# A transformer pair in float32 on one core: nine-instruction roots, a gather of 96 columns, and the gate row of each feed forward at its end

## What is computed

```python
def modulate(x, g, shift, scale):
    return rmsnorm(x, g) * (1.0 + scale) + shift

x = x + g1 * o
x = x + g2 * swiglu(modulate(x, n_ffn, sh2, sc2), wg, wu, wd)

def swiglu(h, wg, wu, wd):
    return (jax.nn.silu(h @ wg) * (h @ wu)) @ wd
```

## Time and profile before

| | |
|---|---|
| median of 3 runs | 2700.8 us (2697.67 to 2712.5) |
| profiled execution: its time, its span | 2701.12 us, 2698.8 us |
| PE busy, share of the span | 2443.1 us, 91% |
| DVE busy | 1892.0 us, 70% |
| ACT busy | 1472.7 us, 55% |
| HBM read | 671.79 MB |
| TensorE clock granted, mean | 0.957 |

### The profile page before, as it was taken

How to read it: one execution, slowest core, us unless ns; L and a number is a source line. 1 busy time by engine, 2 the same in 40 slices (tenths; PEclk the granted TensorE clock), 3 DMA queues, 4 the chain that set the end, 5 groups by cost and what they waited for, 6 DMA issues and landing times. The chain is left out here.

```text
span 2698.8 us, 58018 instructions
## 1 busy us (share of the span) xinstructions
PE 2443.1 (91%) x22896; PEld 1854.2 (69%) x22998; DVE 1892.0 (70%) x2521; ACT 1472.7 (55%) x1865; POOL 14.9 (1%) x12
## 2 busy tenths in 40 slices
PE   5978999999888879989999999898999999999997
PEld 4745777677664457768677768567777777777775
DVE  3277555555545566555666555669999999999997
ACT  3146444443321545433454434358887888888885
POOL 0000000000200000000000000000000000000000
PEclk9989999999798899999799999789999999999999
DMA  7340555554466126545375545339999999999995
GB/s 293 116 202 24 225 204 195 210 209 148 148 230 244 61 98 250 206 179 201 118 265 196 208 158 207 113 138 357 414 415 403 418 416 413 418 417 418 418 417 227
DMA packets 121210, 674.35 MB, mean 250 GB/s; under 512 B 13488, under 2 KB 13968, under 8 KB 67088
## 3 DMA queue, kind: packets, MB, share of 16 engines
q1 hardware_dynamic: 120032, 664.47, 63.6%
q10 hardware_dynamic: 1072, 8.42, 0.9%
HBM read 671.79 MB, written 1.05 MB: 249 GB/s over the span
## 5 line engine op out<-in xcount | busy, mean ns | idle before, releaser
L959 PE MATMUL ps<-projected,normed_or_mix 128*128 128x256 bf16 x1504 | 409.9, 273 | 1.2 <-issue 1.2
L960 PE MATMUL ps<-projected,normed_or_mix 128*128 128x256 bf16 x1504 | 409.9, 273 | 0.0
L1345 DVE TENSOR_TENSOR aux<-weights,aux 128x1024 bf16<-128x1024 f32 x224 | 273.2, 1220 | 1.4 <-ACT aux L1289 1.4
L1340 DVE TENSOR_TENSOR normed_or_mix<-weights,normed_or_mix 128x2048 bf16<-128x2048 f32 x111 | 254.4, 2292 | 15.5 <-ACT normed_or_mix L1283 10.5
L1340 DVE TENSOR_TENSOR turned<-weights,turned 128x2048 bf16<-128x2048 f32 x112 | 256.6, 2291 | 7.0 <-ACT turned L1283 2.3
L1283 ACT ACTIVATE turned<-weights 128x2048 bf16<-128x2048 f32 x112 | 213.8, 1909 | 52.6 <-DMA weights<-moe 52.6
L1283 ACT ACTIVATE normed_or_mix<-weights 128x2048 bf16<-128x2048 f32 x111 | 212.0, 1910 | 50.8 <-DMA weights<-moe 48.1
L1213 PE MATMUL ps<-projected,normed_or_mix 128*128 (+1 forms) x1792 | 234.5, 207 | 3.3 <-DVEq L1370 3.3
L1289 ACT ACTIVATE aux<-weights 128x1024 bf16<-128x1024 f32 x224 | 233.5, 1043 | 2.1 <-PE ps L1227 1.8
L1214 PE MATMUL ps<-projected,normed_or_mix 128*128 (+1 forms) x1792 | 234.5, 207 | 0.0
L1215 PE MATMUL ps<-projected,normed_or_mix 128*128 (+1 forms) x1792 | 234.5, 207 | 0.0
(11 more groups left out here) (385 smaller groups left out, 5905.7 us busy)
## 6 DMA issues: line engine op xcount, KB each, us to landing
weights<-moe SPq DMA_DIRECT2D x224, 1024.0 KB, 8.5
weights<-moe SPq DMA_DIRECT2D x224, 512.0 KB, 6.6
weights<-l_ffn SPq DMA_DIRECT2D x66, 1024.0 KB, 5.2
weights<-ada SPq DMA_DIRECT2D x64, 1024.0 KB, 5.6
weights<-l_ffn SPq DMA_DIRECT2D x66, 512.0 KB, 5.5
weights<-ada SPq DMA_DIRECT2D x64, 512.0 KB, 6.1
weights<-ffn SPq DMA_DIRECT2D x28, 1024.0 KB, 5.1
weights<-w_in SPq DMA_DIRECT2D x24, 948.0 KB, 4.6
```

The costliest lines, as they stand in the source:

```text
L959: pe.matmul(o, hi, h_hi(k), start=(k == 0), stop=False)
L960: pe.matmul(o, hi, h_lo(k), start=False, stop=False)
L1340: dve.tensor_tensor(gu4[j % SLOTS][1], RING[:, slot(j), 0:2 * D], gu4[j % SLOTS][0], ALU.subtract).then_inc(front_used.sem, 1)
L1345: dve.tensor_tensor(down4[j % SLOTS][1], RING[:, slot(j), 2 * D:3 * D], down4[j % SLOTS][0], ALU.subtract).then_inc(back_used.sem, 1)
```

## The change

The root becomes nine instructions: a first guess with another constant, one Newton step with another factor, and a last step of higher order; the first of the nine is no longer awaited. `modulate` ahead of a feed forward no longer has `gates`. `ffn_parts` makes the gate row itself: PE's 8 matmuls go ahead of the last down, into banks 6 and 7, ACT copies them behind the last silu, and DVE waits for the copy before it multiplies the first bank. At a feed forward's head the order on ACT and DVE becomes input half, gate, input half, up; PE starts with the first half of the input and the gate, and the matmuls of the condition go ahead of the zeros. In the choice of experts the places are 96 instead of 128 (384 columns a gathering matmul instead of 512), and ACT and DVE cast the gate and up of step 1 and the down of step 0 there instead of in the block of the loop.

```diff
-GUESS = 1597463007.0
+GUESS = 1597815328.0
+ROOT = 1.5 ** 0.2
+NEAR = 1.5849084
...
     def rsqrt(dve, r, v, u):
 
-        dve_step(dve, dve.tensor_scalar(r.bitcast(I32), v.bitcast(I32), -0.5, GUESS, ALU.mult, ALU.add))
+        dve.tensor_scalar(r.bitcast(I32), v.bitcast(I32), -0.5, GUESS, ALU.mult, ALU.add)
         dve_step(dve, dve.tensor_scalar(v, v, -0.5, None, ALU.mult))
-        for i in range(3):
+        for near in (True, False):
             dve_step(dve, dve.tensor_tensor(u, r, r, ALU.mult))
             dve_step(dve, dve.tensor_tensor(u, u, v, ALU.mult))
-            last = dve.scalar_tensor_tensor(out=r, in0=u, scalar=1.5, in1=r, op0=ALU.add, op1=ALU.mult)
-            if i < 2:
-                dve_step(dve, last)
-        return last
+            if near:
+                dve_step(dve, dve.scalar_tensor_tensor(out=r, in0=u, scalar=NEAR, in1=r, op0=ALU.add, op1=ALU.mult))
+        dve_step(dve, dve.scalar_tensor_tensor(out=u, in0=u, scalar=ROOT ** 2 * 5 / 3, in1=u, op0=ALU.add, op1=ALU.mult))
+        return dve.scalar_tensor_tensor(out=r, in0=u, scalar=ROOT ** 4 * 1.25, in1=r, op0=ALU.add, op1=ALU.mult)
...
             for k in range(KD):
+                if by_half and w == 0 and k % (KD // 2) == 0:
+                    pe.wait_ge(S.h_lo.sem, S.h_lo.at(k // (KD // 2) + 1))
...
         def products(pe):
+            for i in range(ada_n):
+                ada_row(pe, i, ada_at)
             for bank in range(4):
                 pe.matmul(PS[:, bank, :], Z16[:, 0:PB], Z16[:, :], start=True, stop=False)
...
-            for i in range(ada_n):
-                ada_row(pe, i, ada_at)
             zero_products(pe, 2 if ada_n else 14, 5)
-            pe.wait_ge(S.h_lo.sem, S.h_lo.at(2))
+            if gates is not None:
+                pe.wait_ge(S.h_lo.sem, S.h_lo.at(2))
...
             for c in range(rounds * SLOTS, n):
                 if c + 1 < n:
                     up(c + 1, c + 1)
+                elif gates is None:
+                    pe.wait_ge(S.ada_out.sem, S.ada_out.at(ada_n))
+                    gate_products(pe, row_gates, 6)
                 down_products(pe, c, c, outs, stop=(c == n - 1), each=S.bank_done if c == n - 1 else None)
...
+            if gates is None:
+                keep_gate(act, 0, row_gates, 6)
             squares(act)
...
+            dve.wait_ge(S.gate_kept.sem, S.gate_kept.at(1))
             for b in range(2):
...
-    modulate([(X, 0, 3, 0), (XC, 0, 3, 1)], col("n_ffn", 0, KD), batch=1,
-             gates=[(gate_row, 0, 5, 0), (ctx_gate, 0, 5, 1)])
-    ffn(X, F0, 0)
-    ffn(XC, F0, T, ctx_gate, first=2)
+    modulate([(X, 0, 3, 0), (XC, 0, 3, 1)], col("n_ffn", 0, KD), batch=1)
+    ffn(X, F0, 0, (0, 5, 0))
+    ffn(XC, F0, T, (0, 5, 1), first=2)
...
-                        mm = pe.matmul(PS[:, 4 * part + q % 4, :], tok[:, b, k * PB:(k + 1) * PB],
+                        mm = pe.matmul(PS[:, 4 * part + q % 4, 0:4 * CAP], tok[:, b, k * PB:(k + 1) * PB],
...
                 make_lo(dve, 0, 0, 0)
+                dve.wait_ge(S.hi_gu.sem, S.hi_gu.at(2))
+                dve.tensor_tensor(second_gu[1], second, second_gu[0], ALU.subtract).then_inc(front_used.sem, 1)
+                dve.wait_ge(S.hi_d.sem, S.hi_d.at(1))
+                dve.tensor_tensor(first_down[1], back, first_down[0], ALU.subtract).then_inc(back_used.sem, 1)
                 dve.wait_ge(S.made.sem, S.made.at(1))
...
                 cast_hi(act, 0, 0, 0, free=False)
+                arrived(act, place.n + 1)
+                act.activation(second_gu[0], second, ACT.Copy).then_inc(S.hi_gu.sem, 1)
+                arrived(act, place.n)
+                act.activation(first_down[0], back, ACT.Copy).then_inc(S.hi_d.sem, 1)
```

More of the change, by code:

```diff
@@ L533, in mean_square, with gate_products @@
                                         op0=ALU.add, op1=ALU.add)
-    def gate_products(pe, gates):
+    def gate_products(pe, gates, bank=0):
         for g, (dst, layer, part, c) in enumerate(gates):
             for k in range(KD):
-                mm = pe.matmul(PS[:, 2 * g + k // 4, k % 4 * PB:(k % 4 + 1) * PB],
+                mm = pe.matmul(PS[:, bank + 2 * g + k // 4, k % 4 * PB:(k % 4 + 1) * PB],
                                ADA[:, layer, part * KD + k, c:c + 1].broadcast_to([PB, PB]), ident,
@@ L1009, in ffn_done, with ffn_parts @@
             s.done(n)
-    def ffn_parts(x, f, o, gates=None, gate=GB, first=0, ada_at=None, ada_n=0):
+    def ffn_parts(x, f, o, gates=None, own_gate=None, first=0, ada_at=None, ada_n=0):
         a, n = place.n, f // PB * (NE if gates is not None else 1)
@@ L1022, in ffn_parts @@
         halves = (slice(0, KD // 2), slice(KD // 2, KD))
+        gate, row_gates = GB, own_gate and [(GB[:, :], *own_gate)]
         def products(pe):
+            for i in range(ada_n):
+                ada_row(pe, i, ada_at)
             for bank in range(4):
@@ L1053, in silus @@
         def silus(act):
-            for half in halves:
+            for i, half in enumerate(halves):
                 act.activation(h_hi[:, half, :], h[:, half, :], ACT.Copy).then_inc(S.h_hi.sem, 1)
+                if gates is None and i == 0:
+                    act.wait_ge(front_in[place.n % SLOTS].sem, 16 * (place.n // SLOTS + 1))
+                    act.activation(gu[0][0][:, 0:D], RING[:, place.n % SLOTS, 0:D], ACT.Copy).then_inc(S.w_hi.sem, 1)
             if gates is None:
-                act.wait_ge(front_in[place.n % SLOTS].sem, 16 * (place.n // SLOTS + 1))
-                act.activation(gu[0][0][:, 0:D], RING[:, place.n % SLOTS, 0:D], ACT.Copy).then_inc(S.w_hi.sem, 1)
                 act.activation(gu[0][0][:, D:2 * D], RING[:, place.n % SLOTS, D:2 * D],
@@ L1154, in cast_hi_loop, with ffn @@
             act.activation(split[parity(j)][2][0], RING[:, s, 2 * D:3 * D], ACT.Copy).then_inc(S.hi_d.sem, 1)
-    def ffn(x, f, o, gate=GB, first=0):
+    def ffn(x, f, o, own_gate, first=0):
         a, n, beside = place.n, f // PB, 2
         place.n += beside
-        products, silus, gating = ffn_parts(x, f, o, gate=gate, first=first, ada_at=a, ada_n=beside)
+        products, silus, gating = ffn_parts(x, f, o, own_gate=own_gate, first=first, ada_at=a, ada_n=beside)
         with nc.Block() as block:
@@ L1300, in product_hi @@
                                ACT.Copy).then_inc(S.act_hi.sem, 1)
-            gate_up(1, 1, False)
-            down(0, 0, False)
             gate_up(2, 2, False)
@@ L1371, in gating @@
             dve.sem_inc(S.prod.sem, 2)
-            gate_up(1, 1)
-            down(0, 0)
             gate_up(2, 2)
@@ L2250, in gathered_tile @@
             half, k = q // KD, q % KD
-            return ((HEH, HEL)[part][:, 4 * half:4 * half + 4, k, :],
-                    PS[:, 4 * part + q % 4, :].rearrange("p (e q) -> p e q", e=4))
+            return ((HEH, HEL)[part][:, 4 * half:4 * half + 4, k, 0:CAP],
+                    PS[:, 4 * part + q % 4, 0:4 * CAP].rearrange("p (e q) -> p e q", e=4))
+        second_gu = [XC[:, h, :].bitcast(BF16) for h in range(2)]
+        first_down = [AUX[:, h * 512:(h + 1) * 512].bitcast(BF16) for h in range(2)]
+        second, back = RING[:, (place.n + 1) % SLOTS, 0:2 * D], RING[:, place.n % SLOTS, 2 * D:3 * D]
         with nc.Block() as block:
@@ L2379, in turn_put @@
                 for b in range(2):
[L2380 removed]
+                    t = pe.transpose(PS[0:CAP, e // 2, e % 2 * T + b * PB:e % 2 * T + (b + 1) * PB],
+                                     put[b][:, e, 0:CAP], ident)
                 if e % 2:
@@ L2396, in spread_gates, with move_casts @@
                     mm.then_inc(S.spread.sem, 1)
+            gate_products(pe, general_gate, 6)
             pe.wait_ge(S.spread_kept.sem, 4)
+        def move_casts(dve):
+            for h in range(2):
+                dve.tensor_copy(down[0][h], first_down[h]).then_inc(S.casts_moved.sem, 1)
+            dve.wait_ge(S.casts_moved.sem, 2)
+            for h in range(2):
+                dve.tensor_copy(gu[1][h], second_gu[h]).then_inc(S.casts_moved.sem, 1)
         def keep_spread(act):
+            act.wait_ge(S.casts_moved.sem, 4)
             for i in range(4):
```

49 lines of the change are left out of this document (28 added, 21 removed).

## The result

| | before | changed |
|---|---|---|
| median of 20 runs each | 2704.8 us | 2711.4 us |
| ratio of changed to before | | 1.0029, 95% interval 1.0020 to 1.0039 |
| span of the profiled execution | 2698.8 us | 2709.1 us |
| TensorE clock granted, mean | 0.957 | 0.946 |

A forecast was written before the change was run, and what follows sets the result against it. It took TensorE to bound the feed forwards and DMA of weights the expert loop; terms -2.0 - 2.1 + 8.8 - 1.4 - 0.2 - 2.0 = +1.1 gave 2702 us, range 2693 to 2711.

The forecast's parts named there:

- Step 1: Shorter roots: 0.5 us saved a root, four of sixteen on the path, -2.0 us.
- Step 2: Modulations without gate rows: transposes start sooner, -0.6 or -0.7 us each, -0.1 ahead of the experts; sum -2.1, bounds 0 and -4.
- The rival of the clock: TensorE's clock falls in heads behind longer pauses, about 2.4 us each; 2705 to 2707 with one or two; 15%.
- the heaviest case: Heads and modulations of three feed forwards and the experts' gather all at low clock: 14.4 us, 2716; 4% of the 15.
- a low clock in a head that had 2.4 GHz: Sign in the new profile that the prediction would be wrong.
- Step 3: Gate row ahead of the last down: first gate multiply 2.2 us later in each of four feed forwards, +8.8 us.
- Step 4: Feed forward heads by halves: 0.45 us sooner in each of three heads, -1.4 us in all.
- Step 5: Choice of experts: subtractions +3.3 us on the logits' chain, narrower gather -3.3, narrower copy and placement -0.2; sum -0.2.
- Step 6: Start of the expert weight stream: three loads may go at once instead of one, -2.0 us, bounds 0 and -3.8.

The follow-up runs named there:

- roots_alone: The kernel before with the shorter roots alone; ratio to before 0.9992 (0.9982 to 1.0002).
- gates_left_out: The kernel before without gate products and gate row copies in the three modulations ahead of the feed forwards, nothing in their place; ratio to before 1.0034.
- casts_back: The changed kernel with the two casts and two subtractions back at the start of the experts' loop; ratio to before 1.0053.
- unused_products: The changed kernel with gate products back in all four modulations, results unread, the gate row still made at the feed forward's end; ratio to before 1.0009.
- head_alone: The kernel before with only the new feed forward head (condition's products first, input and weights by halves); ratio to before 0.9992.
- gather128: The changed kernel with gather, picks and copies at 128 columns an expert again, casts and subtractions still early; ratio to before 1.0046.
- warm2: The changed kernel with gate rows back in the modulations, zero products in TensorE's pauses and six more ahead of the router's products; ratio to before 0.9957.

## Why the prediction was wrong, step by step

**Step 1, roots: right, as far as the runs can tell.** At the same place the stretch is 1.72 us for 2.25, so 0.53 a root for the 0.5 of the sum. In roots_alone the stretches that begin at three of the four roots are 0.52, 0.74 and 0.53 shorter; the fourth, ahead of the experts, shows 0.02 only. The runs give 2.2 us for 2.0, with an interval that reaches 1.

**Step 2, the modulations without gate rows: this is the step that failed.** It has -2.1 with 0 as its upper bound ("the transposes run at the lower clock instead"). gates_left_out, which does this step alone for the four feed forwards, measured +9.2. The bound looked only at the transposes. The clock stays low through the head behind them: in layer 1 of the changed kernel the 32 condition products cost 2.56 us more (5.35 for 2.79). The -0.1 ahead of the experts fails too: without the subtractions, casts_back still has the logits 3.5 us later, behind router products at 1.2 GHz. That the missing gate products are the whole cause there is not shown, since unused_products brings the stretch back only to +2.87.

**The rival of the clock had the mechanism, and was priced and weighed too low.** It gave 2705 to 2707 for one or two heads, 2716 for the heaviest case, and 15% in all; the 2711.4 lies between. Three heads were hit, each with 13.7 to 17.1 us at 1.2 GHz in its stretch, where the rival priced one more interval, and the router's products with them. And layer 0 shows what the prediction itself named as a sign of being wrong, a low clock in a head that had 2.4 GHz. The sentence that misled is the one on layer 1's modulation: 0.55 with the gate products in it, read as "they did not hold it up". The products ran at the low clock, and the clock rose as they ended, 0.3 us ahead of the transposes. What they did shows only in the rows behind them, which rows 10 did not hold, as the 2.79 of the condition's products. The Trainium skill's rule ("TensorE: Matmul & The Clock Gate", section "What's actually happening"), that activity releases the throttled state, was cited for it and then set aside by that sentence; gates_left_out and unused_products agree with the rule.

**Step 3, the gate row at the end: right.** The four stretches grew by 2.20, 2.19, 2.20 and 2.20; the sum of 8.8 is met. The products took 1.95, the copy 1.02, and the multiply waits for the copy.

**Step 4, the head by halves: right where the clock is the same**, 0.45 and 0.47 in head_alone. The third head, that of layer 0, is not settled (+1.12, with 3.4 us more at 1.2 GHz), and the runs of head_alone cannot tell 1.4 us from nothing. In the changed kernel step 4 is buried under step 2.

**Step 5, the choice of experts: one term right, one right by accident.** The gather gives 3.3, as forecast. The 3.3 on the logits came as 4.0, near the figure by luck: the subtractions without most of the low clock are 2.4, and the low clock, which the step did not have, would give 3.5 without them. The step's -0.2 came as -1.4, since less of the gather ran at 1.2 GHz (3.4 us for 8.9): gather128, with as short a stretch at 1.2 GHz and the wide gather, still gains 2.1.

**Step 6, the start of the stream: right in kind, its size open.** The rows that answer to the earlier trace rows, and SP's loads, before and changed:

```profile
1838.00:1846.00 8.00, 6.60 (x101) 6.62 (x101) 5.32 (x3) 7.24 (x8) 0.00 (x0) 0.79 0.91 337
1846.00:1870.00 24.00, 22.52 (x375) 18.72 (x373) 21.78 (x19) 20.03 (x21) 0.00 (x0) 1.00 0.92 361
```

```profile
1823.49 5.62 SPq L311 DMA_DIRECT2D weights<-moe  x2
1829.92 0.34 SPq L317 DMA_DIRECT2D weights<-moe  x1
```

```profile
1837.86 1.02 SPq L314 DMA_DIRECT2D weights<-moe  x2
1839.15 0.34 SPq L320 DMA_DIRECT2D weights<-moe  x1
```

The third load is issued 1.3 us behind the first, where it was 6.4, and the share of the first 8 us is 0.91 for 0.66: 2.0 us of transfer. The loop is 3.6 shorter in this profile. But over the profiles of kernels that start the same way it stands between -4.1 (warm2) and +3.1 (gather128), with 6.7 and 16.5 us at 1.2 GHz in it, so one profile does not size it. At 6.2 to 6.8 us at 1.2 GHz the two loops with the early casts stand at -3.6 and -4.1 and the two without at 0 and -0.3; at 10.0 to 10.2 the two with them stand at -1.6 and +0.5, the two without at +0.2 and -0.4. The runs of casts_back put casts and start together at some 6 us, with a wide interval.

**The sum.** With step 2's -2.1 replaced by the 9.2 of gates_left_out, the forecast's +1.1 becomes 12.4; with the 1.2 and 1.6 us more that the profile shows for steps 5 and 6 it becomes 9.6. The runs say 7.8, the profile 10.3. That sum was made afterwards, and the 9.2 alone is uncertain by 3.5 either way.

## What to carry to other kernels

Before taking TensorE work out of a pause, or moving it from there, read the granted clock and the durations of the same instruction behind the pause, not inside it: work that seems free may be what has the next stage run at 2.4 GHz. A stage on which TensorE is the bound pays for the move twice here: 2.2 us a feed forward for the row itself, and 2 to 5 us for the head behind the emptied pause. And where rows show 1.2 GHz behind a pause on the critical path, a few products of zeros into a bank that nobody reads, short enough to end inside the pause, are worth a try: here 0.23% on the kernel before, and 0.43% together with the good parts of this change.

## What the hardware showed that was not expected

Less work was slower: 64 recorded matmuls and four copies fewer cost 0.34%. The gate products of layer 1 run mostly at 1.2 GHz themselves (3.46 us for 1.95), and yet without them the modulation and head are 2.3 us longer, and the next 32 products take 5.35 us for 2.79 (changed kernel) or 4.20 (gates_left_out). Low stretches also lie at different places in different profiles where nothing was changed: the stretch ahead of the modulation of layer 1 (from its second head norm's root) has the same code in eight of these kernels, with 23.9 to 37.5 us at 1.2 GHz, and its length differs by up to 4.4 us. With effects of 1 to 3 us, single profiles are therefore read by stretches with like clock, and the ratio of many runs decides.
